# Attention logits issued head by head in a two-layer float32 trunk on one NeuronCore

## What is computed

```python
proj = h @ w_in                       # q, k, v and one forget gate per head
log_f = jax.nn.log_sigmoid((f_logit + b_f).astype(jnp.float32))
c = jnp.cumsum(log_f, axis=1).transpose(0, 2, 1)
...
logits = jnp.einsum('bhqd,bshd->bhqs', q_i, k).astype(jnp.float32) * scale
logits = logits + c_i[..., :, None] - c[:, :, None, :]
mask = pos_q[:, None] >= pos_k[None, :]
logits = jnp.where(mask[None, None], logits, NEG_INF)
p = jax.nn.softmax(logits, axis=-1).astype(v.dtype)
return jnp.einsum('bhqs,bshd->bqhd', p, v)
```

## Time and profile before

| what | us |
|---|---|
| runs of the kernel before (3) | 1321.86, 1325.40, 1331.17 |
| median | 1325.4 |
| the profiled execution (the third of these) | 1331.17 |
| its span in the profile | 1329.1 |
| outside the span | 2.1 |
| one pass of the attention loop | 9.76 |

### The profile page before, as it was taken

One profiled execution on the slowest core, in us unless ns is written; L12 is line 12 of the kernel. 1 busy time (PEld: TensorE's weight loads), 2 busy tenths in 40 slices (PEclk: granted clock), 3 DMA queues, 4 the chain that ended last, 5 costly groups with the idle time before them and its releaser, 6 DMA issues.

```text
span 1329.1 us, 17417 instructions
## 1 busy us (share of the span) xinstructions
PE 1236.6 (93%) x6640; PEld 894.9 (67%) x6640; DVE 708.0 (53%) x798; ACT 553.9 (42%) x524; POOL 104.2 (8%) x110
## 2 busy tenths in 40 slices
PE   8899999899897999997899999889999979999985
PEld 8799998788786888532588843368883337887332
DVE  5744444656557888300598810078871027885103
ACT  4433343455523777100577700077750026774001
POOL 0000000000000600010040010031001005000101
PEclk9899999999898999999899999999999999999998
DMA  9955555452253899899999999999999999999994
GB/s 305 289 187 174 184 190 173 113 160 96 96 173 128 315 377 371 329 407 402 390 394 393 404 340 410 398 390 394 395 409 363 405 397 393 394 398 374 393 402 176
DMA packets 175640, 414.66 MB, mean 312 GB/s; under 512 B 8704, under 2 KB 48640, under 8 KB 175488
## 3 DMA queue, kind: packets, MB, share of 16 engines
q1 hardware_dynamic: 174608, 409.79, 83.4%
q0 software_dynamic: 960, 3.80, 0.9%
HBM read 412.52 MB, written 1.05 MB: 311 GB/s over the span
## 4 chain that ended last, share of the span: by engine, by line
PE 76%; DMA 12%; DVE 5%; SPq 3%; issue 2%; ACT 2%; DVEq 0%; ACTq 0%
PE bank L1164 19%; PE bank L1166 19%; PE bank L1165 19%; PE bank L1440 9%; DMA raw<-in_moe_w_gate 6%; DMA raw_extra<-in_moe_w_down 5%; PE bank L1453 3%; SPq L435 2%; PE bank L1398 1%; PE bank L1248 1%; DVE w_lo L729 1%; PE bank L1501 1%; ACT w_hi L490 1%; DMA raw<-in_pool_w 1%; PE bank L1346 1%
## 5 line engine op out<-in xcount | busy, mean ns | idle before, releaser
L729 DVE TENSOR_TENSOR w_lo<-raw,w_hi 128x2048 fp32r<-128x2048 f32 x162 | 369.5, 2293 | 142.2 <-ACT w_hi L490 142.0
L490 ACT ACTIVATE w_hi<-raw 128x2048 fp32r<-128x2048 f32 x162 | 310.0, 1916 | 215.9 <-PE bank L1166 144.5
L1164 PE MATMUL bank<-w_hi,h_hi 128*128 128x512 f32 (+1 forms) x848 | 302.9, 357 | 33.0 <-DVE h_lo L1079 14.4
L1166 PE MATMUL bank<-w_hi,h_lo 128*128 128x512 f32 (+1 forms) x848 | 297.3, 351 | 0.0
L1165 PE MATMUL bank<-w_lo,h_hi 128*128 128x512 f32 (+1 forms) x848 | 297.1, 350 | 0.0
L1164 PEld LDWEIGHTS bank<-w_hi,h_hi 128*128 128x128 f32 x848 | 165.4, 195 | 59.4 <-DVE w_lo L729 19.3
L1166 PEld LDWEIGHTS bank<-w_hi,h_lo 128*128 128x128 f32 x848 | 165.1, 195 | 20.4
L1165 PEld LDWEIGHTS bank<-w_lo,h_hi 128*128 128x128 f32 x848 | 165.6, 195 | 18.9
L1440 PE MATMUL bank<-raw,h_b 128*64 128x512 f32 (+1 forms) x864 | 166.5, 533 | 10.1 <-DMA raw<-in_moe_w_gate 6.4
L729 DVE TENSOR_TENSOR w_lo<-raw_extra,w_hi 128x2048 fp32r<-128x2048 f32 x56 | 131.7, 2358 | 18.0 <-ACT w_hi L490 18.0
L1440 PEld LDWEIGHTS bank<-raw,h_b 128*64 128x64 f32 x864 | 60.0, 137 | 107.8 <-issue 90.0
(11 more groups left out here) (227 smaller groups left out, 1171.5 us busy)
## 6 DMA issues: line engine op xcount, KB each, us to landing
raw<-in_moe_w_up SPq DMA_DIRECT2D x88, 1024.0 KB, 12.5
raw<-in_moe_w_gate SPq DMA_DIRECT2D x84, 1024.0 KB, 11.7
raw_extra<-in_moe_w_down SPq DMA_DIRECT2D x60, 1024.0 KB, 14.9
raw<-in_moe_w_down SPq DMA_DIRECT2D x52, 1024.0 KB, 13.6
raw_extra<-in_moe_w_gate SPq DMA_DIRECT2D x28, 1024.0 KB, 10.8
raw_extra<-in_moe_w_up SPq DMA_DIRECT2D x24, 1024.0 KB, 12.8
raw<-in_ffn_w_gate SPq DMA_DIRECT2D x11, 1024.0 KB, 5.8
raw<-in_ffn_w_up SPq DMA_DIRECT2D x11, 1024.0 KB, 5.4
```

The costliest lines, as they stand in the source:

```text
L490: nc.scalar.activation(w_hi[:, slot, :], raw_slot(source), ACT.Copy).then_inc(hi_ready, 1)
L729: nc.vector.tensor_tensor(w_lo[:, slot, :], raw_slot(source), w_hi[:, slot, :].bitcast(f32), ALU.subtract).then_inc(lo_ready, 1)
L1164: mm(out, a_hi, b_hi, start=first, stop=False)
L1166: return mm(out, a_lo, b_hi, start=False, stop=last)
```

## The change

The logits of a pair are issued head by head and no longer block by block. Before, each block had the q-k matmuls of both heads and then the head_row matmuls of both. Now head 0 has both blocks, each q-k matmul followed by its head_row matmul, and then head 1 the same. `s_psum` is raised for head 0 in the middle of the eight matmuls rather than at the last but one. The wait for `mx_done` of the pair before, one wait for both heads, becomes one wait ahead of each head. No other engine's program changes.

```diff
-                if j > 0:
-                    pe.wait_ge(mx_done, 2 * (j - 1) + 2)
-
-                def logits(i, b):
-                    return bank[1 + i][:, b * P:b * P + (b + 1) * P]
-
-                for b in range(TB):
-                    for i in range(2):
-                        h0 = i * HD
-                        mm(logits(i, b), qk[h0:h0 + HD, b * P:(b + 1) * P], qk[h0:h0 + HD, T:T + (b + 1) * P],
+                for i in range(2):
+                    if j > 0:
+                        pe.wait_ge(mx_done, 2 * (j - 1) + i + 1)
+                    h0 = i * HD
+                    for b in range(TB):
+                        to = bank[1 + i][:, b * P:b * P + (b + 1) * P]
...
+                        mm(to, qk[h0:h0 + HD, b * P:(b + 1) * P], qk[h0:h0 + HD, T:T + (b + 1) * P],
                            start=True, stop=False)
-                    for i in range(2):
-                        step = mm(logits(i, b), head_row[:, 2 * j + i, :], ncT2[:, 0:(b + 1) * P], start=False,
-                                  stop=True)
-                        if b == TB - 1:
-                            step.then_inc(s_psum, 1)
+                        step = mm(to, head_row[:, 2 * j + i, :], ncT2[:, 0:(b + 1) * P], start=False, stop=True)
+                    step.then_inc(s_psum, 1)
```

## The result

| | median us | runs | against before |
|---|---|---|---|
| before | 1328.3 | 4 (1321.9 to 1331.3) | |
| changed | 1346.6 | 4 (1341.8 to 1347.0) | 1.0141, interval 1.0119 to 1.0162 |
| changed, second time, before at 1329.6 | 1348.3 | 4 (1346.5 to 1350.1) | 1.0138, interval 1.0115 to 1.0160 |

The change makes the kernel 1.4% slower, 18 to 19 us. The forecast was 1335 with a range up to 1343, and "within 1%" as the likeliest case. The profiled execution of the changed kernel took 1346.0 us with a span of 1343.9, which is 14.8 more than the span before.

The account below looks back on a forecast made before the run. TensorE's issued work was taken to bound the attention loop. The 1325.4 us median plus 9.8 (passes 1 to 7) and 0.6 (last pass), less 1.0 for the clock at the loop's end, gave 1334.8, called 1335; range 1328 to 1343.

Parts of the forecast that it names:

- within 1%: Whole program: time indistinguishable from no change, within 13.3 us either way; chance 0.72.
- the price of the order: Logits of a pass: lost head pairing and doubled row-mode changes take 3.17 us against 1.77, +1.40 a pass.
- the 0.21 which the prediction put on top of the streaming: Logits on TensorE: each change between 64 and 80 rows costs about 0.21 us, unhidden weight load plus empty time.
- Sum at an unchanged clock: Attention loop and its end: 9.8 us for passes 1 to 7 plus 0.6 for the last, +10.4 us.
- rival B: Attention loop: granted clock falls inside passes, 1.5 to 2.5 us each, program 1341 to 1352 us; chance 0.12.
- head 0 at the end: Last pass: head 0's transposes start 0.11 us earlier, counted from the start of the logits.
- the forecast of the gaps: Last pass: TensorE's 2.63 us gap shrinks to about 1.4, a second over a microsecond opens between the heads' transposes.
- one microsecond taken off for the end of the loop: Loop's end: clock falls again three times in four, so a quarter of its 3.7 us cost, 1 us, is subtracted.
- the time that the sum starts from: Whole program before the change: 1325.4 us, median of the three runs shown.
- A: Logits: only the head pairing is lost, +0.64 us a pass, about +4.5 in all, 1330 us; chance 0.12.
- D: Logits: order makes no difference, head 1's q-k runs beside head 0's 80-row matmul, 1326 us; chance 0.02.
- C: Loop's end: head 0's earlier release closes the gap, clock never falls, switches cost nothing, faster, 1325 us; chance 0.04.

Follow-up runs that it names:

- heads_bunched: Kernel before with logits head by head, each head's two q-k blocks then its two head_row matmuls, second blocks in own banks: 1334.4 us, ratio 1.0042.
- pairs_bunched: Kernel before with both heads' q-k side by side for both blocks, then all four head_row matmuls, second blocks in own banks: 1327.3 us, ratio 0.9970.
- heads_then_gates: Kernel before with head 0's q-k blocks, then head 1's, then all four head_row matmuls, second blocks in own banks: 1324.1 us, one execution.
- all_but_last: Kernel before with the changed order in passes 1 to 7 only, the last pass in the old order: 1344.3 us, one time.
- after_filled: Changed kernel plus two keep_warm filler matmuls per pass where TensorE waits for pT, ahead of the logits: 1345.9 us, ratio 1.0125.
- before_filled: Control: kernel before plus the same two keep_warm filler matmuls per pass at the wait for pT: 1331.1 us, ratio 1.0002.

## Why the prediction was wrong

**Right: the price of the order.** The groups of one pass came out within 0.02 us of the prediction, 3.13 us where 3.17 stood; a pass without a fall is +1.38 for +1.40, and the last pass is +0.6 for +0.64. Loop and end at an unchanged clock: 7 x 1.38 + 0.6 = 10.3 us against the 10.4 of the sum. The three other orders fit the same model: 2.46 us for heads_bunched as computed, 1.42 and 1.43 for the two with one change of rows, 0.02 to 0.07 above what it gave. The rule of the Trainium skill (TensorEngine Tiling (Array Packing), Key Properties) that a change of tiling mode drains the engine agrees with these rows, which put about 0.17 us on each change that is taken away (0.67 us for four between the changed kernel and heads_bunched, 0.35 for two between the kernel before and pairs_bunched). That is less than the 0.21 which the prediction put on top of the streaming; head_row matmuls one behind the other still take 0.14 us each (0.56 for four in pairs_bunched). The page's statement that different tiles can work in parallel agrees too (0.86 us for two heads, 0.84 for one), and heads_then_gates shows that the two heads' matmuls need not be neighbours in the program.

**Wrong: the step "Sum at an unchanged clock".** The clock inside the loop was put at nothing in the sum and left to rival B with a chance of 0.12. This is the step of the mechanism that failed. The argument against B was that the present passes hold thin stretches too and kept the clock. The runs showed the opposite. With 3.13 us of logits in a row, 3 of the first 7 passes meet a fall, in each of the four profiles whose loop has this order without fillers in the logits (12 of 28). No pass does in the eight profiles whose loop has an order of at most 2.46 us (0 of 56), though these passes come at different spacings (9.42, 9.76 and 10.46 us). Each fall costs 1.49 us, the lower end of what B gave (1.5 to 2.5), so the missing term is 3 x 1.49 = 4.5 us. B itself named its point: it "decides against me from two such passes on".

So it is shown that this order of the logits brings the falls. That it does so by their thinness (small matmuls with gaps between them) is argued and not shown. For it: all 12 falls begin 2.93 to 3.74 us behind the start of a pass's logits, which is around the end of their 3.13 us, and each lasts 3.4 us; fillers ahead of the logits leave three falls, two between the heads leave one, and one behind each of three head_row matmuls leaves none. But passes with the same instructions meet a fall in one case and not in the next. The falls stand in passes 2, 4 and 7 in one profile of the changed kernel, in 2, 4 and 6 in the other and in all_but_last, in 2, 5 and 7 in after_filled: never in neighbours, always two or three passes apart. So the time at which the logits come seems to decide as well (argued from this spacing), and fillers inside the logits change that too, since they lengthen the pass from 11.14 to 11.57 and 11.91 us. With one profile each, the one fall and the none can come from either. Fillers of the same length at another place of the pass, or more profiles, would tell them apart; neither was run.

**Wrong in one detail: head 0 at the end.** "After the change head 0's transposes start 0.11 us earlier" left out that head 1's reduction is ahead of head 0's reciprocal on VectorE. They start 0.33 us later. With that the forecast of the gaps was off as well: 1.59 us before the first transposes for "about 1.4", and 0.25 before the second for "over a microsecond". Head 1's transposes, which set the end, came at 6.03 us for a computed 6.06, so the sum did not suffer.

**Wrong: one microsecond taken off for the end of the loop.** "I expect it to fall again three times in four". It fell in both profiles of the changed kernel, with a mean clock of 0.70 and 0.68 in the stretch, so nothing was to be taken off for these.

**Too low: the time that the sum starts from.** The forecast starts from 1325.4 us, the median of three runs that lie 9 us apart. With one run more the median of the kernel before is 1328.3, and over 17 to 25 runs on each of three chips 1329.3 to 1330.4. With the falls in and the microsecond back, the sum is 1325.4 + 10.3 + 4.5 = 1340.2, still inside the range; from 1328.3 it is 1343.1, at its edge. The rest up to the measured 1346.6, 3.5 us, is open. So the wrong mechanism alone does not put the time outside the range.

**The other rivals.** A fell with the pass of +1.38 us where it had +0.64, and with heads_bunched. D (no difference) and C (faster) never had a row for them.

**What stays open.** The trace accounts for 14.7 us. The two comparisons of medians say 18.3 and 18.7 us, with intervals of about 15 to 22. The 4 us between them I can't assign, and part of them may be scatter: after_filled, whose attention stage costs 14.9 us more by its profile, came out at 15.5 us. From the output projection to the end of the span it took 966.0 us before and 968.2 and 970.4 in the two profiles of the changed kernel, but 962.7 to 971.8 over the profiles of all fourteen kernels, whose code is the same there; one execution of each does not separate a small effect of the change from that scatter.

## What to carry to other kernels

Where small matmuls of different row counts alternate on TensorE, price each switch from the trace and put those of one kind together: here the same eight matmuls took 1.42, 1.77, 2.46 or 3.13 us by their order (at 1.42 and 2.46 us with banks of their own for the second blocks). An earlier signal is worth nothing to an engine that no one waits for, so look up first who waits. And where a change makes a stretch longer in which the array is fed in small pieces, read the granted clock there and put it into the sum, not beside it: one fall of three microseconds costs as much as a pass's whole reordering.

## What the runs showed that was not expected

- Four records of one head on 64 rows take 0.84 us, eight records of two heads on the two halves of the array 0.86, and it makes no difference whether the heads alternate or come one behind the other.
- A signal that comes earlier for one head can make that head later: head 0's reciprocal waited on VectorE behind head 1's reduction, and its transposes came 0.33 us later.
- The clock at the loop's end is not the same each time in the order of before: in the profile of the kernel before it was low from 357.8 to 368.0 us, well into the output projection, and in that of before_filled back at 1.00 at 359.7, before the projection began at 361.0.
- Twenty-four matmul records put into a wait of 2.63 us kept the clock at 1.00 through the output projection and gave 3.2 us in the two stages, while four records ahead of the thin logits left the three falls of the loop.
